# Odd layer of a two-layer attention block: index scores two heads at a time between the steps of keys and values, and the sums and factors of the head norms in side-by-side pairs

## The reference, cut to what matters

```python
def odd_layer(hn, rel_bias, w_in, w_out, q_g, k_g):
    q, k, v, gate, qi, ki, wi = split_cols(hn @ w_in, ODD_SPLITS)
    q = rms_norm(q.reshape(bsz, L, C_HEADS, C_HEAD_DIM), q_g)       # 8 heads of 128
    k = rms_norm(k.reshape(bsz, L, C_KV_HEADS, C_HEAD_DIM), k_g)    # 2 heads of 128
    ...
# dsa_attention, for one block of 128 queries
rel = relu(einsum('bqhd,bsd->bqhs', qi_blk, ki) * (IDX_DIM ** -0.5))   # 8 index heads of 64
score = einsum('bqhs,bqh->bqs', rel, w_blk)
score = where(key_pos <= t, score, NEG_INF)
_, idx = lax.top_k(score, topk)                                        # 256 of up to 1024
```

## Time and profile before

| what | us |
|---|---|
| median of 3 runs | 2109.1 |
| all three runs | 2109.01, 2109.1, 2120.7 |
| the profiled execution's own time | 2109.57 |
| its span, first to last instruction | 2108.3 |
| TensorE busy in the span | 2022.3 (96%) |
| VectorE busy | 1410.3 (67%) |
| ScalarE busy | 873.4 (41%) |
| mean granted TensorE clock | 0.988 of full |

### The profile page before, as it was taken

One profiled execution on the slowest core, in us unless ns is written; L12 is line 12 of the kernel. 1 busy time (PEld: TensorE's weight loads), 2 busy tenths in 40 slices (PEclk: granted clock), 3 DMA queues, 4 the chain that ended last, 5 costly groups with the idle time before them and its releaser, 6 DMA issues.

```text
span 2108.3 us, 24436 instructions
## 1 busy us (share of the span) xinstructions
PE 2022.3 (96%) x9260; PEld 1536.7 (73%) x9260; DVE 1410.3 (67%) x2159; ACT 873.4 (41%) x1524; POOL 653.2 (31%) x484
## 2 busy tenths in 40 slices
PE   8999989999999999899999999999999989999997
PEld 6778856787557676566678787888787667778885
DVE  7668676422346889445517699899998756784649
ACT  5333276333445662344412333444224544362431
POOL 3676520552101112345434000000003544235443
PEclk9999999999999999999999999999999999999999
DMA  6422330442401112311043211121133112556322
GB/s 259 134 58 77 109 118 21 170 140 76 135 20 41 41 51 80 100 41 50 21 170 114 86 42 60 32 79 50 60 110 117 64 55 73 193 190 219 110 81 110
DMA packets 72429, 197.91 MB, mean 94 GB/s; under 512 B 11182, under 2 KB 20559, under 8 KB 71800
## 3 DMA queue, kind: packets, MB, share of 16 engines
q1 hardware_dynamic: 72168, 196.35, 27.2%
q10 hardware_dynamic: 144, 0.00, 0.0%
HBM read 152.89 MB, written 46.71 MB: 95 GB/s over the span
## 4 chain that ended last, share of the span: by engine, by line
PE 60%; DVE 16%; ACT 4%; issue 3%; POOL 2%; DMA 2%; SPq 0%; DVEq 0%; ACTq 0%; POOLq 0%
PE psum L262 57%; DVE m L2878 3%; PE psum L265 3%; POOL m L307 1%; DMA m<-in_w 1%; DVE m L2899 1%; DVE m L2111 1%; PE psum L1984 1%; ACT m L297 1%; DVE m L317 1%; DVE m L536 1%; DVE m L452 1%; DVE m L527 1%; DVE m L3070 1%; DVE m L3051 1%
## 5 line engine op out<-in xcount | busy, mean ns | idle before, releaser
L262 PE MATMUL psum<-m,m 128*128 128x512 f32 (+8 forms) x8420 | 1920.8, 393 | 51.9 <-DVE m L2235 10.6
L262 PEld LDWEIGHTS psum<-m,m 128*128 128x128 f32 (+4 forms) x8420 | 1443.0, 187 | 503.3 <-issue 157.6
L307 POOL TENSOR_TENSOR m<-m,m 128x1024 fp32r<-128x1024 f32 (+1 forms) x122 | 309.0, 2537 | 1023.1 <-ACT m L297 1022.7
L297 ACT ACTIVATE m<-m 128x1024 fp32r<-128x1024 f32 (+2 forms) x166 | 173.6, 1049 | 355.0 <-PE psum L262 222.7
L2878 DVE SCALAR_TENSOR_TENSOR m<-m,m,m 128x1024 f32<-128x1024 f32 x240 | 310.2, 1294 | 6.3
L265 PE MATMUL psum<-m,m 128*128 128x128 f32 x784 | 110.5, 277 | 20.3 <-ACT m L2399 5.7
L265 PEld LDWEIGHTS psum<-m,m 128*128 128x128 f32 x784 | 90.5, 142 | 40.8 <-ACT m L1431 10.6
L2111 DVE TENSOR_SCALAR_CACHE_REDUCE m<-m,m 128x896 bf16<-128x896 f32 (+4 forms) x130 | 102.7, 847 | 1.0
L2235 DVE CUSTOM_DVE_ANT_0 m<-psum,m 128x128 f32<-128x128 f32 (+3 forms) x64 | 48.2, 754 | 55.2 <-POOL m L2436 21.5
L2436 POOL TENSOR_TENSOR m<-m,m 128x384 f32<-128x384 f32 (+5 forms) x48 | 72.2, 1525 | 11.3 <-DVE m L2235 11.3
L2341 ACT ACTIVATE m<-m,m 128x1024 bf16<-128x1024 f32 (+1 forms) x62 | 64.1, 1037 | 23.6 <-DVE m L2138 23.6
(11 more groups left out here) (305 smaller groups left out, 1649.4 us busy)
## 6 DMA issues: line engine op xcount, KB each, us to landing
m<-in_w SPq DMA_DIRECT2D x164, 512.0 KB, 3.5
scr_hscr<-m SPq DMA_DIRECT2D x4, 2048.0 KB, 6.6
m<-scr_hscr SPq DMA_DIRECT2D x4, 2048.0 KB, 10.9
...
```

Source lines behind the costliest of these rows:

```text
L262: return self.nc.tensor.matmul(out, lhsT, rhs, start=start, stop=stop, skip_group_check=True)
L297: k.nc.scalar.activation(k.hi[SLOT[i]][:, 0:kk * n], k.raw[i % 2][:, 0:kk * n], ACT.Copy).then_inc(*k.up("w_hi", i))
L307: k.nc.gpsimd.tensor_tensor(lo, raw, hi.bitcast(F32), ALU.subtract).then_inc(*k.up("w_lo", i))
```

## The change

Five things change, all in the odd layer.

1. The scores are taken in pairs (`twos`): for one query block, one pair of heads and one chunk of keys, the even head in the upper half of the array's rows and the odd head in the lower half, one directly after the other, into two banks. The ring `mis` has four banks instead of three, `rel` four buffers instead of two (the two new ones lie where query head 7 is put later, so that its raw copy waits for the last score).
2. The pairs are no longer put between whole half panels but between single steps of keys and values, a step being the three matmuls of one slice: three steps first, then the turn of wi, then one step after each of the first 29 pairs and two after each of the last 11. The 42 steps that are left follow without scores.
3. The sums of squares of both halves go into one bank, into partitions 0 to 31 and 32 to 63 (32 columns of ZS each), and `sum_square` is called once per head, after the first half panel of the next one: ten calls of two matmuls.
4. Root and reciprocal are taken once over [64, 512]; `norm` issues the two halves of a head directly after each other, from partitions 0 to 9 and 32 to 41, into two banks: ten calls of two matmuls.
5. The rounds of the bisection follow the scores: five of them are dealt out between the last six copies of the values (`lead`), the others at 3 rounds per two half panels (before: 29 per 20), so that they end at half panel 17 and not 22; `settle` comes at 18 instead of 22, the picks at 19 to 24 instead of 23 to 28.

The diff, cut to what the prediction speaks of:

```diff
-        self.rs = k.tile(H0 + 8 * KB, [1024])
+        self.rs = k.tile(H0 + 8 * KB, [512])
...
-        self.held = ((3, ("free", "od_x0", "on_t", 0, 7)), (4, ("free", "od_x1", "on_t", 1, 4)))
-        self.mis = Ring(k, "od_mis", [5, 6, 7], [("free", "od_x1", "on_t", 1, 5 + i) for i in range(3)])
-        self.rel = Ring(k, "od_rel", [k.tile(H0 + 20 * KB + 2 * KB * i, [512]) for i in range(2)])
+        self.held = (3, ("free", "od_x0", "on_t", 0, 7))
+        self.mis = Ring(k, "od_mis", [4, 5, 6, 7], [("free", "od_x1", "on_t", 1, 4 + i) for i in range(4)])
+
+        self.rel = Ring(k, "od_rel", [k.tile(o, [512]) for o in (H0 + 20 * KB, H0 + 22 * KB, PH + 28 * KB, PH + 30 * KB)])
...
-        self.chain = [("score", b, h) for b in self.order for h in range(8)]
+        self.twos = [(b, i, c, e) for b in self.order for i in range(4) for c, e in self.chunks(b)]
...
+        self.ahead, n = 3, 3
+        steps = [("ok", m, half) for m in range(2) for half in range(2) for _ in range(8)] + [("ov", b) for b in range(8) for _ in range(8)]
+        self.beside, self.over = [], {}
+        for p in range(len(self.twos)):
+            self.beside.append(1 if n < 32 else 2)
+            for j in range(n, n + self.beside[-1]):
+                if j % 8 == 7:
+                    self.over[p] = steps[j]
+            n += self.beside[-1]
+        self.left = [steps[j] for j in range(n, len(steps)) if j % 8 == 7]
+
+        self.chain = []
         for i in range(32):
             self.chain += [("count", i, b) for b in self.by_dve + self.by_act] + [("bits", i)]
 
-        done = [min(32, (29 * (u + 1)) // 20) for u in range(32)]
-        self.deal = [7 * (b - a) for a, b in zip([0] + done, done)]
-
-        self.norms = [(n, half) for n in (8, 0, 1, 2, 3, 4, 5, 6, 7, 9) for half in range(2)]
+        self.lead = [6] * (len(self.left) - 1) + [35 - 6 * (len(self.left) - 1)]
+        done = [min(32, 5 + (3 * (u + 1)) // 2) for u in range(32)]
+        self.deal = [7 * (b - a) for a, b in zip([5] + done, done)]
+
+        self.norms = [8, 0, 1, 2, 3, 4, 5, 6, 7, 9]
...
+    def heads(self, half):
+
+        return slice(32 * half, 32 * half + 10)
...
+    def sum_square(n):
+
+        pe.wait_ge(*at("zs"))
+        pe.wait_ge(*at(*O.held[1]))
+        for half in range(2):
+            pe.wait_ge(*at("head_sq", n, half))
+            ins = k.mm(k.bank(O.held[0])[32 * half:32 * half + 32], O.ZS[:, 9 - n:41 - n], O.sq[half], n == 8, n == 7)
+        ins.then_inc(*up("head_ss", n))
+
+    def keys_values():
+
+        for m in range(2):
+            for half in range(2):
+                hs = slice(512 * half, 512 * half + 512)
+                bank = k.bank(O.proj.take("ok", m, half))
+                pe.wait_ge(*O.proj.freed("ok", m, half))
+                wh, wl = pe_panel(k, f"ok{m}")
+                for kk in range(8):
+                    ins = k.mm3(bank, (wh[:, kk, :], wl[:, kk, :]), (k.XH[:, kk, hs], k.XL[:, kk, hs]), kk == 0, kk == 7)
+                    if kk < 7:
+                        yield
+                ins.then_inc(*up("head_ps", 8 + m, half, also=[done(f"ok{m}")] if half else ()))
+                if (m, half) == (1, 0):
+                    sum_square(8)
+                yield
+        for b in range(8):
+            bs = slice(128 * b, 128 * b + 128)
+            bank = k.bank(O.proj.take("ov", b))[:, 0:256]
+            pe.wait_ge(*O.proj.freed("ov", b))
+            for i in range(2):
+                wh, wl = pe_panel(k, f"ov{i}")
+                for kk in range(4):
+                    j = 4 * i + kk
+                    ins = k.mm3(bank, (k.XH[:, j, bs], k.XL[:, j, bs]), (wh[:, kk, :], wl[:, kk, :]), j == 0, j == 7)
+                    if j < 7:
+                        yield
+            ins.then_inc(*up("ov_ps", b, also=[done("ov0"), done("ov1")] if b == 7 else ()))
+            if b == 0:
+                sum_square(9)
+            yield
+
+    steps = keys_values()
+    for _ in range(O.ahead):
+        next(steps)
+    bank = k.bank(O.mis.take("wi"))
+    pe.wait_ge(*O.mis.freed("wi"))
...
+    for p, (b, i, c, e) in enumerate(O.twos):
+        pe.wait_ge(*at("qi", i, b // 4))
+        for half in range((e - 1) // 512 + 1):
+            pe.wait_ge(*at("ki", half))
+            pe.wait_ge(*at("ki_up", half))
+        banks = [k.bank(O.mis.take("score", b, 2 * i + j, c)) for j in range(2)]
+        for j in range(2):
+            pe.wait_ge(*O.mis.freed("score", b, 2 * i + j, c))
+        for j in range(2):
+            hl = slice(64 * j, 64 * j + 64)
+            k.mm(banks[j][:, 0:e - c], O.QI[hl, i, 128 * b:128 * b + 128], O.KI[hl, c:e], True, True).then_inc(*up("score_ps", b, 2 * i + j, c))
+        for _ in range(O.beside[p]):
+            next(steps)
+    for _ in steps:
+        pass
...
+            if late is not None and half == 0:
+                sum_square(late)
+        late = m
...
+    def norm(n):
+
+        banks = [k.bank(O.mis.take("norm", n, half)) for half in range(2)]
+        for half in range(2):
+            pe.wait_ge(*O.mis.freed("norm", n, half))
+        pe.wait_ge(*at("head_rt"))
+        for half in range(2):
+            hs = O.heads(half)
+            ins = k.mm(banks[half], k.ident[hs, hs.start + n:hs.start + n + 1].to_broadcast([10, 128]), O.rs[hs], True, True)
+        ins.then_inc(*up("head_norm", n))
...
-    def score(b, h):
+    for b, i, c, e in O.twos:
         sc, n = O.SC[b], 128 * (b + 1)
-        wv = O.WI[:, b, h:h + 1]
-        for c, e in O.chunks(b):
-            rb = O.rel[("score", b, h, c)][:, 0:e - c]
+        for h in (2 * i, 2 * i + 1):
+            rb, wv = O.rel[("score", b, h, c)][:, 0:e - c], O.WI[:, b, h:h + 1]
...
-        step(2)
+    step = Walk(O.chain, count=own, bits=bits)
...
         if u == 18:
+            dve.wait_ge(*at("head_ms"))
+            V.reciprocal(O.rs[0:64], O.rs[0:64]).then_inc(*up("head_rt"))
+        for n in O.norms_after(u - 16):
             for half in range(2):
-                rs = O.rs[0:10, 512 * half:512 * half + 512]
-                dve.wait_ge(*at("head_ms", half))
-                V.reciprocal(rs, rs).then_inc(*up("head_rt", half))
-        for head in O.norms_after(u - 16):
-            norm(*head)
-        if u == 22:
+                norm(n, half)
+        if u == 18:
             settle()
-        if 23 <= u < 29:
+        if 19 <= u < 25:
             for part in range(2):
-                pick(u - 21, part)
+                pick(u - 17, part)
...
+        if n == 7:
+            act.wait_ge(*at("score", 2))
...
+    for p, (b, i, c, e) in enumerate(O.twos):
+        for h in (2 * i, 2 * i + 1):
+            rb = O.rel.take("score", b, h, c)[:, 0:e - c]
+            act.wait_ge(*O.rel.freed("score", b, h, c))
+            act.wait_ge(*at("score_ps", b, h, c))
+            A.activation(rb, k.bank(O.mis[("score", b, h, c)])[:, 0:e - c], ACT.Relu, scale=0.125 * 2.0 ** 90).then_inc(
+                *up("rel", b, h, c, also=[("free", "od_mis", "score", b, h, c)]))
+        if p - 1 in O.over:
+            key_value(*O.over[p - 1])
+    step = Walk(O.chain, count=signs)
+    for n, use in zip(O.lead, O.left):
+        step(n)
+        key_value(*use)
...
+                act.wait_ge(*at("head_ss", 7))
+                A.activation(O.rs[0:64], k.bank(O.held[0])[0:64], ACT.Sqrt, bias=k.epsc[0:64, 0:1], scale=1.0 / 128).then_inc(*up("head_ms"))
```

107 lines of the change are left out of this document (21 added, 86 removed).

## The result

| what | before | after |
|---|---|---|
| median, runs side by side | 2114.74 (4 runs) | 2077.44 (4 runs) |
| ratio, 95% interval | | 0.9825 [0.9803, 0.9847] |
| profiled execution | 2109.57 | 2075.31 |
| its span | 2108.3 | 2074.1 |
| end of ki to the queries (oq) | 107.6 | 93.5 |

The forecast was 2078 with a range of 2071 to 2089. The forecast starts from the profiled execution of before, 2109.57, which lies near the fast end of that kernel's executions (2108.37 to 2121.67 in all the runs here), while those of the changed kernel lie between 2074.36 and 2079.62; so the medians are further apart, 37.3 us, than the two profiled executions, 34.3.

The account below looks back on a forecast made before the run. TensorE was taken to bound the stage; savings of 12.9 (scores, keys, values), 9.4 (sums of squares) and 9.2 us (norms), 31.5 in all, off the profiled 2109.57 gave 2078, range 2071 to 2089.

Parts of the forecast that it names:

- Scores, keys and values: TensorE from the end of ki to the queries: 94.3 us instead of 107.2, saving 12.9 us.
- The three steps ahead: Steps of keys before the turn of wi: fill 1.4 us idle; the clock may stay up, otherwise some 1.7 us return.
- Edges: Entries into half-array mode on TensorE: 0.22 us each, forty of them 8.8 us, already counted in the pairs' 45.4.
- Sums of squares: In oq and og, a pair in two column groups costs what a single one does: 8 x 1.18 = 9.4 us saved.
- The second rival: Column pairs of the sums of squares run one after the other: 8.7 us missing, 2087; chance 0.05.
- Norms: In og, a head's two norms side by side in different row groups, plus 0.7 of bank waiting: 9.2 us saved.
- The slack of one microsecond at head 0: In oq, ACT squares head 0 by 653.4, TensorE needs it at 654.5; if DVE is 3 late, one 2 us wait.
- The bisection and the tail: Rounds start near 624 and end about 748, ahead of the first norm at 761; og's tail shifts unchanged.
- The sum: The three savings together: 12.9 + 9.4 + 9.2 = 31.5 us off the profiled 2109.57.
- ACT and DVE hold TensorE: Relu loop, head copies or stretched rounds delay TensorE at pairs or first heads: 4 to 11 us lost, 2082 to 2089; chance 0.14.
- The gain was not given back: Rival: bisection rounds stretch about 1 us each, TensorE waits 20 us or more before its first norm: 2098 to 2110; chance 0.06.
- The clock rival: Small alternating pieces drop the granted clock to 1.2 GHz in the stretch of pairs, up to 2172; chance 0.03.

Follow-up runs that it names:

- experiment 5: Changed kernel without the three steps of keys ahead of the turn of wi; 2081.54, ratio 0.9843 to the kernel before.
- experiment 7: Changed kernel with bisection rounds dealt as before the change and the pairs put in blocks instead of between steps; 2088.98, ratio 0.9872.
- experiment 12: Changed kernel with a step between the two heads of each pair and seven steps ahead of the turn of wi, not three; 2134.28, ratio 1.0105.
- experiment 11: Changed kernel with both products of each pair taken from the upper half of the rows, so the result differs; 2154.96, ratio 1.0223.
- experiment 4: Changed kernel with two pairs of scores in a row, then two steps of keys or four of values; 2073.58, ratio 0.9802.
- experiment 1: Changed kernel with the sums of squares taken one half at a time again; 2087.73, ratio 0.9869.
- experiment 2: Changed kernel with both halves of each norm contracting over partitions 0 to 63, the same row groups; 2087.16, ratio 0.9872.
- experiment 8: Changed kernel with two pairs in a row and one bisection round moved from the second half panel of queries to the third; 2070.54, ratio 0.9788.
- experiment 6: Changed kernel with the bisection rounds dealt out as before the change; 2076.06, ratio 0.9818.
- experiment 10: Changed kernel run and profiled once more, unaltered; 2077.65, ratio 0.9828.
- experiment 9: Changed kernel with a step of keys or values between the two heads of each pair; 2164.45, ratio 1.0193.

## Why the prediction was right

**Scores, keys and values: 12.9 us, measured 14.1.** The stretch was to go from 107.2 to 94.3 and went from 107.6 to 93.5. A pair and a step were priced at 1.96 and take 1.95. Of the 1.2 us that the sum missed, 0.4 is where the stretch before is cut, and 0.8 are small overstatements of the price of a pair, up to 0.03 each in the keys and 0.05 in the values (1.95 with two steps, 2.0 forecast). The three steps ahead are worth 3.3 us (experiment 5). The sum held both parts of it, the 1.4 of idle time and the 1.7 of clock, since it had full speed throughout; that the clock would stay up was hoped for and not derived, and it did. The split of the remaining gain can't be added up from undoing: side by side alone, in blocks, gives 1.0 us (experiment 7 against before; up to 7.8 by the estimate with the clock up), and interleaving without it gives less than nothing (137.0 against 107.6 with the clock up, experiment 12; 118 by estimate, experiment 11). The two pay in full only together: a pair in 1 us outruns DVE's 1.61 unless other work stands behind it, and steps between scores that run in turn only add edges.

**Edges: 0.22 each, in part too small.** The Trainium skill (TensorEngine Tiling (Array Packing), Key Properties) says that a change of tiling mode drains the engine; the trace agrees, and experiment 4 prices a removed entry at 0.39 us in the keys and 0.27 over all 20, 5.4 us together. Part of that is the overlap of the second pair with the first and no edge, and no run separates a drain from it. In the sum this did no harm, because pair and edges were taken from rows as a whole; where it mattered is that it left 5 us on the table.

**Sums of squares: 9.4 us; experiment 1 loses 8.4 in the second stretch**, where it also avoids a wait of 1.3 us, so 9.7 without it. The second rival is out: the pair costs what the single costs. The Trainium skill (TensorE: Matmul & The Clock Gate, Part 3, The mechanism) says that loads overlap running matmuls only where the row group differs, and a few lines ahead names the background weight buffer as another way, which the prediction left out; the trace of column groups does not agree with the narrow rule, with four loads in 0.14 us and 0.98 to the next product. It agrees where rows and columns are both shared: in experiment 2 the loads go in turn.

**Norms: 9.2 us, measured by experiment 2 as 8.5**, the row groups alone. The 0.7 for waiting on a bank stands once in the trace of before, as the prediction counted it; no run takes the fourth bank away to test it.

**The slack of one microsecond at head 0: the term that was missing.** The prediction named this place, with 1 us of slack, and a wait of 2 if DVE were late by 3. It waited 1.3. DVE's first count came at 621.9, 2.1 ahead of the forecast, and the sum's first loads at 651.9, 2.6 ahead of it, so the slack was half a microsecond. Then the eighth round's counts began on ACT at 650.59, 28.7 us behind DVE's first count and not 7 x 3.80 = 26.6: the 2.1 us are DVE's one slow operation beside POOL. The Trainium skill (SBUF — State Buffer, SBUF: two separate sides) states a rule for it that I had not applied: a DVE instruction with two inputs in SBUF and a GpSimd instruction that reads SBUF lock each other out, and whichever starts second waits for the whole of the first. The trace agrees, 2.30 us against 0.18. No experiment took it away by itself, and where the slack is larger it does little harm: in experiments 5 and 8 it takes 2.28 us as well, and TensorE waits 0.2 and 0.5. The second stretch saved 17.3 and not 18.6; experiment 6, where the wait is gone whole, saves 18.7.

**The bisection and the tail.** The first count, the start of oq, the gate's end at 833.9 (836 forecast, with everything 1.6 earlier from upstream) and the attention behind it shifted as forecast; no wait of TensorE for DVE of over 0.4 us stands in og. The earlier rounds were not needed for that (experiment 6).

**The sum.** 31.5 forecast, 323.4 less 292.0 = 31.4 measured in the stage. That it is so close is partly luck: 1.2 us too little in the first stretch and the wait of 1.3 in the second cancel. The profiled execution fell by another 2.8 us outside the stage. The rows of experiment 10 put that down to the clock in the rest of the kernel: two falls of 3.4 us are missing, and in its own execution, where two others have come in, the rest is 1784.4, near the 1784.9 of before. The medians fell by 37.3, and the traces account for 31.4 of it. Of the kernel before only one execution was profiled; its executions have mean granted clocks from 0.990 (2108.37) down to 0.982 (2121.67), those of the changed kernel 0.988 to 0.990. So the kernel before usually lost more to the clock than its profile shows. Where it did, and whether the change removes it, is not shown; worked from the median of 2114.74 in place of 2109.57, the same sum would have given 2083.

**The rivals.** ACT and DVE hold TensorE once, 1.3 us, not 4. The gain was not given back by longer rounds. The clock rival was dismissed at 0.03 on the ground that pairs between values ran at full speed. It was right for this kernel and too confident as a reason: two small edits away, experiments 9 and 11 show just that, some 30 to 36 and up to 51 us lost at 1.2 GHz and a kernel slower than before.
